# The opening of a transformer kernel, by blocks of 128 channels

## The reference

```python
c_act = silu(c)
mod = c_act @ ada_w[layer] + ada_b[layer]
sh1, sc1, g1, sh2, sc2, g2, sh3, sc3, g3 = split(mod, 9)
h = rms_norm(x, norm_g[layer, 0]) * (1 + sc1) + sh1
g, u = split(h @ ffn_w_in[layer, 0], 2)
x = x + 0.5 * g1 * ((silu(g) * u) @ ffn_w_out[layer, 0])
```

## Time and profile before

| what | us |
|---|---|
| median of 3 executions (2137.86 to 2140.4) | 2138.07 |
| the profiled execution: own time | 2131.74 |
| its span | 2130.0 |
| TensorE busy | 1784.6 |
| VectorE busy | 1732.5 |
| first product with `h` begins | 45.1 |

### The profile page before, as it was taken

One profiled execution on the slowest core, in us unless ns is written; L12 is line 12 of the kernel. 1 busy time (PEld: TensorE's weight loads), 2 busy tenths in 40 slices (PEclk: granted clock), 3 DMA queues, 4 the chain that ended last, 5 costly groups with the idle time before them and its releaser, 6 DMA issues.

```text
span 2130.0 us, 30921 instructions
## 1 busy us (share of the span) xinstructions
PE 1784.6 (84%) x11480; PEld 1504.6 (71%) x11480; DVE 1732.5 (81%) x3006; ACT 860.7 (40%) x1352; POOL 538.3 (25%) x464
## 2 busy tenths in 40 slices
PE   4999898999999998999999999999655655555565
PEld 4998798999999987899899999989222222221221
DVE  5887777888988888754679998848999989998877
ACT  3443466544555446644455445564212112111101
POOL 0111002111001110211110002422565555445441
PEclk7999999999999998999999999999887678788678
DMA  7889733688868794254545444527999999999996
GB/s 317 316 315 365 297 129 139 247 315 293 295 248 322 299 330 162 102 203 165 181 160 191 166 178 160 197 100 299 412 422 422 422 422 422 422 423 422 422 423 259
DMA packets 88783, 606.25 MB, mean 285 GB/s; under 512 B 9763, under 2 KB 11059, under 8 KB 21468
## 3 DMA queue, kind: packets, MB, share of 16 engines
q1 hardware_dynamic: 37708, 245.03, 31.7%
q0 software_dynamic: 37040, 270.57, 30.6%
q10 hardware_dynamic: 13920, 89.15, 10.4%
HBM read 601.53 MB, written 3.18 MB: 284 GB/s over the span
## 4 chain that ended last, share of the span: by engine, by line
PE 23%; DVE 17%; DMA 16%; issue 3%; ACT 1%; POOL 1%; DVEq 0%; POOLq 0%; ACTq 0%
DMA row_pair<-in_peer_uv,mod_ring 16%; PE ps L806 12%; DVE row_pair L2534 3%; DVE w_lo L1872 3%; PE ps L1291 3%; PE ps L837 2%; DVE XTOK L2553 2%; DVE work L2304 2%; PE ps L938 2%; DVE SQ L2304 2%; PE ps L939 1%; POOL row_pair L778 1%; PE ps L869 1%; DVE work L1929 1%; PE ps L903 0%
## 5 line engine op out<-in xcount | busy, mean ns | idle before, releaser
L1872 DVE TENSOR_TENSOR w_lo<-raw,w_hi 128x2048 fp32r<-128x2048 f32 (+1 forms) x248 | 527.6, 2131 | 192.0 <-ACT w_hi L1313 191.3
L1291 PE MATMUL ps<-row_pair,diag 128*128 128x512 f32 x512 | 353.2, 855 | 269.5 <-ACT diag L1839 269.5
L1313 ACT ACTIVATE w_hi<-raw 128x2048 fp32r<-128x2048 f32 (+1 forms) x248 | 440.2, 1776 | 222.3 <-PE ps L939 72.8
L1291 PEld LDWEIGHTS ps<-row_pair,diag 128*128 128x128 f32 x512 | 135.8, 278 | 486.3 <-ACT diag L1839 324.1
L806 PE MATMUL ps<-HH,w_hi 128*128 128x256 f32 x1584 | 444.9, 281 | 0.7 <-DVE w_lo L1872 0.7
L806 PE MATMUL ps<-HH,w_lo 128*128 128x256 f32 x1584 | 443.1, 280 | 0.0
L806 PE MATMUL ps<-HL,w_hi 128*128 128x256 f32 x1584 | 441.9, 279 | 0.0
L778 POOL DMA_INDIRECT row_pair<-in_peer_uv,mod_ring x256 | 328.9, 1285 | 323.7 <-PE ps L1291 223.1
L2534 DVE SCALAR_TENSOR_TENSOR row_pair<-row_pair,HTOK 128x1024 f32<-128x1024 f32 x256 | 312.0, 1220 | 62.8 <-DMA row_pair<-in_peer_uv,mod_ring 60.4
L806 PEld LDWEIGHTS ps<-HH,w_hi 128*128 128x128 f32 x1584 | 297.0, 188 | 2.5 <-DVE w_lo L1872 1.3
L806 PEld LDWEIGHTS ps<-HL,w_hi 128*128 128x128 f32 x1584 | 297.8, 188 | 0.7 <-issue 0.7
(11 more groups left out here) (325 smaller groups left out, 3004.9 us busy)
## 6 DMA issues: line engine op xcount, KB each, us to landing
raw<-in_f_in SPq DMA_DIRECT2D x88, 1024.0 KB, 4.9
mod_ring<-in_ada ACTq DMA_DIRECT2D x74, 1024.0 KB, 7.1
raw<-in_f_out SPq DMA_DIRECT2D x64, 704.0 KB, 5.6
raw<-in_mix_a SPq DMA_DIRECT2D x16, 1024.0 KB, 4.8
raw<-in_mix_g SPq DMA_DIRECT2D x8, 1024.0 KB, 4.8
raw<-in_pq SPq DMA_DIRECT2D x8, 1024.0 KB, 4.8
first<-in_ada ACTq DMA_DIRECT2D x4, 1024.0 KB, 13.0
raw<-in_a_q SPq DMA_DIRECT2D x4, 1024.0 KB, 6.0
```

What stands on the lines that cost most here:

```text
L1291: last = mm(ps[:, 2 * t + c, :], diag[:, d, :], row_v(k)[:, c * 512:(c + 1) * 512], start=False, stop=False)
L1313: f(slot(w_hi, g), slot(raw, g), ACT.Copy).then_inc(hi_ready, 1)
L1872: v.tensor_tensor(slot(w_lo, g), slot(raw, g), f32(slot(w_hi, g)), ALU.subtract).then_inc(low["v"], 1)
```

## The change

Tile k of the first eight now holds shift and scale of one block k of 128 channels. Even tiles go through VectorE's dots, odd ones through 16 one-column products. SP issues c_row, X, the eight tiles, weight tiles 0 and 1 between the first of them and weight tile 2 behind them, with no wait; the small inputs go to ScalarE's queue. Each block is scaled and shifted by itself, and TensorE takes its part (`open_part`, six products) of weight tiles 0 and 1. The loop over input tiles starts at slot 2 of `f00_in`, modulation tiles 8 and 9 are eaten at slots 0 and 1, and the bias parts 0, 1 and 2 move from the output product to the time before the loop and to slots 20 and 21, parts 3 and 4 to m = 1 and 3 of it. In the diff, hunks follow the file; `...` marks what is left out.

```diff
 def summed(q):
 
-    return q + 1 if q < DIRECT else q
+    return q - OPEN // 2 + 2
 
 
 def eaten(n):
 
-    return n + 1 if n < 2 * DIRECT else n - 1
+    return n - OPEN + 1
 
...
-        first = place("first", WORK_AT + 6 * KF, 4 * TILE)
-        first_more = place("first_more", HH_AT, 2 * TILE)
+        open_at = [MOD_AT, MOD_AT + TILE, *(WORK_AT + 6 * KF + n * TILE for n in range(4)), KS_AT, VS_AT]
+        open_tile = [place(f"open_tile{k}", at_, TILE) for k, at_ in enumerate(open_at)]
...
-            sp.dma_start(onehot[:, :], a["onehot"]).then_inc(small_loaded, 16)
-            sp.dma_start(lamp[:, :], a["a_lambda"].partition_broadcast(P).rearrange("q a n -> q (a n)")).then_inc(small_loaded, 16)
-            sp.dma_start(fgate_b[:, :], a["fgate_b"]).then_inc(small_loaded, 16)
-            sp.dma_start(prm[:, :], a["prm"]).then_inc(prm_loaded, 16)
             sp.dma_start(c_row, a["c_row"].partition_broadcast(P).rearrange("q a n -> q (a n)")).then_inc(c_row_loaded, 16)
             sp.dma_start(X[:, :, :], a["xT"]).then_inc(x_loaded, 16)
-
-            sp.wait_ge(mod_eaten, 2)
 
             def tiles(name, t0=0, n=None, i=None):
...
-                tiles(w_in, 0, RING)
+                if w_in != "f00_in":
+                    tiles(w_in, 0, RING)
...
+            for k in range(OPEN):
+                sp.dma_start(open_tile[k][:, :], a["ada"][k]).then_inc(open_loaded[k], 16)
+                if k < RAW_TILES:
+                    tiles("f00_in", k, 1)
+            tiles("f00_in", 2, 1)
             ffn("f00_in", "f00_out")
...
+            def open_direct(k):
+
+                pe.wait_ge(open_loaded[k], 16)
+                w = open_tile[k][:, :].rearrange("p (k n) -> p k n", k=DC)
+                for m in range(2):
+                    for c in range(DC):
+                        last = mm(ps_direct[:, k - 1 + m:k + m], w[:, c, m * P:(m + 1) * P], c_act[:, c:c + 1],
+                                  start=(c == 0), stop=(c == DC - 1))
+                last.then_inc(direct_ready, 1)
+
+            def open_part(t, k):
+
+                ln = LIN["f00_in"]
+                if k == 0:
+                    tile_wait(ln.tile0 + t)
+                    for m in range(2):
+                        freed_wait(ln.chunk0 + 2 * t + m, None)
+                w = wparts(ln.tile0 + t)
+                outs = [ps[:, BANK[ln.chunk0 + 2 * t + m], 0:SEQ] for m in range(2)]
+                if t == 0:
+                    pe.wait_ge(hh_ready, SET["n0"] + k + 1)
+                for m in range(2):
+                    for u in range(2):
+                        mm(outs[m], w[u][:, k, m * P:(m + 1) * P], HH[:, k, :], start=(k == 0 and u == 0), stop=False)
+                if t == 0:
+                    pe.wait_ge(hl_ready, SET["n0"] + k + 1)
+                for m in range(2):
+                    last = mm(outs[m], w[0][:, k, m * P:(m + 1) * P], HL[:, k, :], start=False, stop=(k == DC - 1))
+                    if k == DC - 1:
+                        last.then_inc(units_done, 1)
+
...
-            for m in range(4):
-                for k in range(DC):
-                    w = mod_ring[:, (k // 4) * TILE:(k // 4 + 1) * TILE].rearrange("p (k n) -> p k n", k=4)
-                    last = mm(ps_direct[:, m:m + 1], w[:, k % 4, m * P:(m + 1) * P], c_act[:, k:k + 1],
-                              start=(k == 0), stop=(k == DC - 1))
-            last.then_inc(direct_ready, 1)
-            ffn(0, "f00_in", "f00_out", "n0", 1, 8)
+            open_direct(1)
+            open_part(0, 0)
+            open_direct(3)
+            open_part(0, 1)
+            open_part(0, 2)
+            open_part(1, 0)
+            open_direct(5)
+            open_part(0, 3)
+            open_part(1, 1)
+            open_part(0, 4)
+            open_part(1, 2)
+            open_direct(7)
+            open_part(1, 3)
+            open_part(1, 4)
+            for k in range(5, DC):
+                open_part(0, k)
+                open_part(1, k)
+            ffn(0, "f00_in", "f00_out", None, 1, 10)
 
...
-
+                if n >= OPEN + 2:
                     act.wait_ge(mod_eaten, at(i, 4, eaten(n - 2)))
+                elif n == OPEN:
+                    act.wait_ge(open_dots, 1)
+                else:
+                    act.wait_ge(direct_ready, 1)
                 src = a["ada"][n] if i is None else a["ada"][bass.ds(i * 4 + n, 1)].rearrange("a p f -> (a p) f")
...
                         f(GUH[:, t, :], graw[:, t % 2, :], ACT.Copy).then_inc(hidden_hi, 1)
+                elif n == 0:
+                    split(ln.tile0 + 2)
+                    for t in range(RAW_TILES):
+                        q = ln.chunk0 + 2 * t
+                        act.wait_ge(units_done, CHUNK_UNIT[q])
+                        f(silu[:, t, :], ps[:, BANK[q], 0:SEQ], ACT.Silu).then_inc(freed["a"], 1)
+                        split(ln.tile0 + t + 3)
+                        act.wait_ge(freed["d"], FREE[q + 1][1])
+                        f(GUH[:, t, :], graw[:, t, :], ACT.Copy).then_inc(hidden_hi, 1)
+                        load_mod(ada + t)
+                    bias_part(0)
...
+                    if n == 0:
+                        bias_part(t - 19)
...
-                    if n == 0 and m < 5:
-                        bias_part(m)
+                    if n == 0 and m in (1, 3):
+                        bias_part((m + 5) // 2)
...
 
-            act.wait_ge(prm_loaded, 16)
-
-            for n in (0, 6, 1, 7, 2, 3, 4, 5):
-                if n < 6:
-                    act.dma_start(first_tile(n), a["ada"][n]).then_inc(first_loaded[n], 16)
-                else:
-                    act.dma_start(mod_ring[:, (n % 2) * TILE:(n % 2 + 1) * TILE], a["ada"][n]).then_inc(mod_loaded[n % 2], 16)
+            act.dma_start(prm[:, :], a["prm"]).then_inc(prm_loaded, 16)
+            act.dma_start(onehot[:, :], a["onehot"]).then_inc(small_loaded, 16)
+            act.dma_start(table[0:NB, :], a["rel_bias"]).then_inc(small_loaded, 16)
+            act.dma_start(lamp[:, :], a["a_lambda"].partition_broadcast(P).rearrange("q a n -> q (a n)")).then_inc(small_loaded, 16)
+            act.dma_start(fgate_b[:, :], a["fgate_b"]).then_inc(small_loaded, 16)
             act.wait_ge(vec_consts, 1)
-            f(c_act[:, :], col("c", 0, DC), ACT.Silu).then_inc(c_ready, 1)
+            step(f(act_scratch[:, :], eps[:, :], ACT.Silu))
             act.wait_ge(c_row_loaded, 16)
             f(c_row, c_row, ACT.Silu).then_inc(c_row_ready, 1)
+            act.wait_ge(prm_loaded, 16)
+            f(c_act[:, :], col("c", 0, DC), ACT.Silu).then_inc(c_ready, 1)
             act.wait_ge(x_loaded, 16)
             for k in range(DC):
                 square(0, k)
             act.wait_ge(units_done, 8)
             f(bias_row, ps[0:A_HEADS, OUT_BANKS[0], :], ACT.Copy).then_inc(line_ready, 1)
             act.sem_inc(freed["a"], 6)
-            act.wait_ge(lam_sum_ready, 1)
-            f(lam_exp[:, :], lam_sum[:, :], ACT.Exp).then_inc(lam_exp_ready, 1)
+            step(f(act_scratch[:, :], eps[:, :], ACT.Sqrt))
+            act.wait_ge(line_ready, 1)
+            act.dma_start(bias_line, bias_row).then_inc(line_written, 16)
             norm_root(0)
             split(0)
-            split(1)
-
-            act.wait_ge(direct_ready, 1)
-            load_mod(8)
-            load_mod(9)
-            act.wait_ge(line_ready, 1)
-            act.dma_start(bias_line, bias_row).then_inc(line_written, 16)
-            shift_high("n0", 0)
+            for k in range(DC):
+                act.wait_ge(t_ready, k + 1)
+                f(HH[:, k, :], SQ[:, k, :], ACT.Identity, bias=mods[:, k:k + 1]).then_inc(hh_ready, 1)
+                if k == 1:
+                    split(1)
+                if k == 3:
+                    act.wait_ge(lam_sum_ready, 1)
+                    f(lam_exp[:, :], lam_sum[:, :], ACT.Exp).then_inc(lam_exp_ready, 1)
+                    step(f(act_scratch[:, :], eps[:, :], ACT.Silu))
+            load_mod(OPEN)
+            load_mod(OPEN + 1)
             act.wait_ge(line_written, 16)
-            ffn(0, "f00_in", "f00_out", 1, 8)
+            ffn(0, "f00_in", "f00_out", 1, 10)
 
             norm_root(1)
             shift_high("n1", 1)
...
-                    dve.wait_ge(mod_loaded[h], at(i, 32, 16 * (n // 2 - 2)))
-                    w = mod_ring[:, h * TILE:(h + 1) * TILE]
-                w = w.rearrange("p (a k) -> p a k", a=2)
...
+                elif n == 0:
+                    for t in range(RAW_TILES):
+                        q = ln.chunk0 + 2 * t
+                        dve.wait_ge(units_done, CHUNK_UNIT[q + 1])
+                        dve.wait_ge(freed["a"], FREE[q][1])
+                        dve.wait_ge(hidden_lo, t + 1)
+                        v.tensor_tensor(graw[:, t, :], ps[:, BANK[q + 1], 0:SEQ], silu[:, t, :], ALU.mult
+                                        ).then_inc(freed["d"], 1)
+                        if t == 0:
```

(79 more changed lines are left out.)

31 lines of the change are left out of this document (10 added, 21 removed).

## The result

The change makes the kernel slower: 2144.69 us against 2136.06 (medians of 15 executions each), ratio 1.0043, 95% interval 1.0032 to 1.0054. The forecast was 2132.7 us, faster. The profiled execution of the kernel after has a span of 2143.3 us and an own time of 2145.09.

What follows compares the result with a forecast made beforehand. Loads then a serial tail bound the opening, TensorE the loop, both the output weights. Gains of 2.7 (opening and loop) and 2.7 us (output) were summed as 5.4: 2131.74 to 2126.3 own time, median 2132.7, range 2125.5 to 2138.

Steps and rivals of the forecast that it cites:

- the price of the one-column products: Opening, TensorE: 16 one-column products per odd block cost 1.8 us at the full clock or 3.5 at half.
- The loads: Opening: same bytes, bound by bandwidth, the last modulation tile at 35.8 us; about 1.3 us won, uncertain by 1 us.
- VectorE's blocks: Opening: adds, gains and scalings per block cost 3.2 us more in all; block 7 done at 40.1 if nothing held it.
- The clock: Opening, TensorE: at half from about 22 us, back at full at 40.3 during four parts of the weight tiles.
- Rival C: Opening: clock stays low until the last run of parts, T0 = 51.7, gain 1.6 us, median 2136.5; chance 0.13.
- The wait ahead of tile 4: First loop: TensorE idles 5.0 us until T0+17.0, start at 64.9 gains 4.8 us, less 2.1 for the clock: 2.7.
- T0: Opening: the time at which TensorE ends weight tile 0, forecast at 47.9 us.
- The output products: Output weights stage: moved bias transfers save 4.9 us of TensorE waits, held load 24 gives back 2.2: 2.7 us gained.
- rival E: Output stage: load 24, held behind the bias write, lands near 183.6; 4.5 us slower, 2142.6 us; chance 0.07.

Runs made afterwards that it cites:

- e2: Changed kernel with 2 one-column products instead of 16 in each of the four phases, so its result is not the one wanted: 2130.91 us, ratio 0.9983 to before.
- e4: Changed kernel with the four small inputs first on SP's queue, ahead of c_row: 2142.05 us, ratio 1.0040 to the kernel before.
- e7: Changed kernel with bias part 2 behind load 24 and VectorE's splits of tiles 4 and 5 ahead of the dots of modulation tiles 10 and 11: 2145.07 us, ratio 1.0054.
- e10: Kernel before without the bytes of the attention bias (four transfers of 2 KB, the last reading another input; bias wrong): 2129.74 us, ratio 0.9978.
- e6: Kernel before with only the attention bias moved: part 0 ahead of the loop, parts 1 and 2 two slots apart: 2135.97 us, ratio 1.0011.
- e12: Kernel before with three VectorE instructions earlier, unread products in two TensorE pauses, and bias transfers on GpSimd's own queue (bias delivered wrong): 2128.46 us, ratio 0.9975.
- e5: Kernel before with three VectorE instructions (reciprocal, low part of weight tile 0) moved ahead of the last loads: 2131.60 us, ratio 0.9986.
- e1: Kernel before again, without an edit, for a second profile: 2137.13 us, span 2135.3 against 2130.0 in the first profile.
- e3: Changed kernel with the five bias parts back at their old places in the output product: 2144.78 us, ratio 1.0051 to the kernel before.
- e11: Changed kernel with four unread fp32 products of 256 columns between the first one-column phase and the first part: 2140.10 us, ratio 1.0030 to before.

## Why the prediction was wrong

**The failed step is the price of the one-column products.** From x64 in the earlier trace rows I read 64 products, and wrote so of the kernel before; the program says 4 columns x 8, so 32, and each fp32 product stands in the trace as two instructions. Sixteen are therefore x32: 3.63 us at the full clock and 6.82 at half, 0.113 and 0.213 an instruction, where I had 1.8 and 3.5 us. My price per instruction was right, the count was half. Four phases: 10.6 us forecast, 18.8 measured.

The first phase cost nothing, because TensorE waited behind it for the low part of weight tile 0 until 24.30; the second began at 26.08 (forecast 25.9). From there on TensorE was the path without a pause, in the forecast and in the trace. The second, third and fourth phase held it for 6.7, 3.6 and 4.5 us up to the next part, where I had 3.5, 3.5 and 1.8: 6.0 us more. The seven parts behind the fourth took 7.15 us in place of 4.9, because the clock was at half until 54.0. With 0.3 us of small differences that is the whole of the 8.5 us by which tile 0 was late, 56.4 in place of 47.9. e2 shows it from the other side.

The weight load probably sets the price and not the column. In the trace of before the loads (PEld) are busy for nearly all of the 10.63 us:

```profile
21.01 10.58 PEld L1139 LDWEIGHTS ps<-c_act,mod_ring 128*128 128x128 f32 x64 [2.07 <-issue]
```

The Trainium skill (TensorE: Matmul & The Clock Gate, LDWEIGHTS) puts the load at its columns over 1.2, an estimate of 107 ns for 128 of them. The trace is near it at the full clock with 113 and far from it at half with 213, and no run separates load and product.

**The loads** were right: DMA share 1.01 until 37.1, and VectorE waits for no modulation tile behind the root. But the small inputs, now behind `prm` on ScalarE's queue, landed at 12.04 us, not at about 5.5, which I had not counted: the root was done at 19.3, not 17.6. e4 took it away, and no gain can be shown.

**VectorE's blocks** came at the expected pace between the waits; block 7 was to be done at 40.1 and came behind the last wait at 49.45. (By my own rows the eight blocks cost VectorE 2.8 us more, not 3.2; nothing hung on it.)

**The clock.** I had it come back once, at 40.3. It was down from 23.3, then it came and went: back at 37.0, down again at 40.4, back at 43.8, down at 47.2, back at 54.0. The first fall lies in the pause behind a one-column phase, the other two at the end of one and within one. (The return 3.1 us after 45.10 that I read in the earlier trace rows was at 48.4, so after 3.3.) Rival C (cold to the end, tile 0 at 51.7) was nearer in time, by another way. The Trainium skill (TensorE: Matmul & The Clock Gate, HAM oscillation), which I had cited, tells of a clock that falls in the waits between bursts of products. That can explain the first fall only: TensorE had no wait from 26.08 us until the one ahead of tile 4.

**The wait ahead of tile 4** was right to 0.2 us: T0+17.0 = 73.40, wait 4.83 (forecast 5.0), and the clock was at half from 71.1 to 77.9, in it and behind it. Only T0 was wrong, so a gain of 4.8 became a loss of 3.7, and 2.0 more by the clock. e2 shows that the wait doesn't come from the one-column products, and in e7, with the order in VectorE's queue changed, the waits of the loop add to more.

**The output products.** I was right that the bias causes the waits (e10), and wrong that moving three parts would save them. Load 24 was held as I described: bias write issued at 167.14, landed by 175.02, load 24 landing at 184.84, near rival E's 183.6; TensorE idled 3.74 us for it, and the later waits were gone. The clock was at half from 187.1 to 194.0 around it and cost what the waits had saved: the stage up to norm 1 took 67.4 us, 67.2 before. The 1.2 us between 4.9 and 3.7 us of waits is in any case less than executions differ by: e4, whose output stage is the program of after, has 1.7 us. e6, e7 and e12 give the load another place in three ways and have 3.5, 4.0 and 4.3 us of waits. What decides there, when two of five transfers remain, is still open.

**The sum.** At the mark: -2.7 forecast for the opening, -2.7 for the output products; measured +3.7 at tile 4, +2.0 from there to the end of the loop, and +0.2 in the output stage and norm 1: +5.85 with roundings. The medians differ by 8.6 (interval of the ratio: 6.8 to 11.5); I can't show where the 2.8 us beyond the mark lie. The two profiles drift 7.5 us further apart there, but mostly by the execution: 3.1 us between 640 and 800 us, with the slow loop, and 2.0 between 600 and 640, where e10, with the program of before, has 1.5.

**The range** left out a loss, and the rivals moved the clock, the waits and the loads but none the price of a phase. Rival E's 2142.6 us is near the measured 2144.7 by luck: load 24 was late as it says, but the 3.4 us that it takes the output stage to lose were not lost, and the loss that came lay in the opening.

## What to carry to other kernels

Before pricing a group of instructions, divide its count in the profile by the count in the program: an fp32 product of one column was two instructions and took 0.23 us at the full clock, 0.43 at half. And an engine that looks idle ahead of the change may be the bound once such work is spread between dense products. Look first whether order alone gives the gain: three instructions moved into waits made the first product 4.35 us earlier (e5), where a new scheme lost time. In the output stage, removing the bytes of the bias took its waits away, and moving a part of them out, mending their order or changing their queue did not.

## What was not expected of the hardware

A loop of 256-column products starts them 0.1175 or 0.1196 us apart with the granted clock at 1.00 in both; it changes between loops of one execution and between executions of one program (e1, and the first loop of e4, e5, e6 and e10 too), 2.0 us in the first loop. What sets it is open. And TensorE's clock fell under one-column phases with the engine busy all the time, twice in the opening of after, in places that changed with each kernel: the same four phases took 18.8, 22.4, 20.9 and 16.5 us in after, e3, e4 and e11 (sums of four rows each).
